# VectorE's order in the projection of a hybrid encoder step: odd side places first, the even place in front of each behind it

## The reference

```python
h = _rms(x, p['norm_gain']) * (1 + scale[:, None, :]) + shift[:, None, :]
(qkv_raw, z_a, beta_raw, alpha_raw, q_raw, ckv_raw, kr_raw, z_b, g_a, g_b) = _split_in(h @ p['w_in'])
o_a, conv_new, s_new = _deltanet(qkv_raw, beta_raw, alpha_raw, conv_buf, s0, p)
o_b, ckv_new, kr_new = _mla(q_raw, ckv_raw, kr_raw, pos, past_ckv, past_kr, p)
```

## Time and profile before

| what | value |
|---|---|
| runs | 1935.47, 1940.38, 1939.29 us; median 1939.29 |
| profiled execution | 1939.42 us, of which the span from first to last instruction 1937.6 us |
| TensorE busy (matmul) | 1806.0 us, 93% of the span |
| VectorE busy | 931.0 us, 48% |
| ScalarE busy | 636.0 us, 33% |
| GpSimd busy | 266.6 us, 14% |
| mean granted TensorE clock | 0.969 |

### The profile page before, as it was taken

One profiled execution on the slowest core, in us unless ns is written; L12 is line 12 of the kernel. 1 busy time (PEld: TensorE's weight loads), 2 busy tenths in 40 slices (PEclk: granted clock), 3 DMA queues, 4 the chain that ended last, 5 costly groups with the idle time before them and its releaser, 6 DMA issues. The chain is left out here.

```text
span 1937.6 us, 28688 instructions
## 1 busy us (share of the span) xinstructions
PE 1806.0 (93%) x11162; PEld 1661.2 (86%) x11162; DVE 931.0 (48%) x1820; ACT 636.0 (33%) x1173; POOL 266.6 (14%) x254
## 2 busy tenths in 40 slices
PE   6899999989888899999999989989999987999898
PEld 2599999989887899999999978878887975999787
DVE  0644455673555486796322144454444556242333
ACT  2322443553433351333333233244333434020100
POOL 0111111434333340241311100000000000000000
PEclk9899999999998999999999989989999987999899
DMA  9322323577775674345654230032251986342222
GB/s 315 116 77 94 102 101 126 170 215 226 221 231 170 184 221 135 126 135 187 214 167 146 112 104 22 28 120 87 77 185 28 368 247 207 131 134 77 100 87 71
DMA packets 235249, 284.06 MB, mean 147 GB/s; under 512 B 42865, under 2 KB 194702, under 8 KB 234988
## 3 DMA queue, kind: packets, MB, share of 16 engines
q1 hardware_dynamic: 233692, 277.82, 44.9%
q10 hardware_dynamic: 1264, 4.39, 0.6%
q0 software_dynamic: 160, 0.05, 0.0%
HBM read 177.30 MB, written 104.92 MB: 146 GB/s over the span
## 5 line engine op out<-in xcount | busy, mean ns | idle before, releaser
L1919 PE MATMUL PS<-HH,WL 128*128 128x352 f32 (+1 forms) x1752 | 392.9, 332 | 4.9 <-DVE mod L2069 4.9
L1919 PE MATMUL PS<-HL,WH 128*128 128x352 f32 (+1 forms) x1752 | 380.6, 326 | 0.0
L1919 PE MATMUL PS<-HH,WH 128*128 128x352 f32 (+1 forms) x1752 | 380.3, 325 | 0.0
L1919 PEld LDWEIGHTS PS<-HH,WH 128*128 128x128 f32 (+1 forms) x1752 | 302.6, 189 | 0.3
L1919 PEld LDWEIGHTS PS<-HH,WL 128*128 128x128 f32 (+1 forms) x1752 | 294.5, 190 | 7.9 <-issue 5.0
L1919 PEld LDWEIGHTS PS<-HL,WH 128*128 128x128 f32 (+1 forms) x1752 | 300.0, 189 | 0.2
L2041 DVE TENSOR_TENSOR WL<-Wraw,WH 128x2048 fp32r<-128x2048 f32 (+1 forms) x37 | 89.7, 2423 | 89.7 <-ACT WH L1691 88.0
L2054 DVE SCALAR_TENSOR_TENSOR R<-R,colA 128x1059 f32<-128x1059 f32 x72 | 99.2, 1378 | 5.9 <-issue 0.5
L1711 ACT ACTIVATE R<-PS 128x1056 f32<-128x1056 f32 (+1 forms) x49 | 51.4, 1050 | 142.4 <-PE PS L1919 142.4
L627 ACT ACTIVATE pr<-PS,amx 128x128 f32<-128x128 f32 (+8 forms) x72 | 51.4, 714 | 132.6 <-DVE amx L661 132.6
L602 PE MATMUL PS<-V,pT 128*128 128x128 f32 (+1 forms) x624 | 86.8, 283 | 3.3 <-ACT pT L639 2.9
(11 more groups left out here) (311 smaller groups left out, 2887.3 us busy)
## 6 DMA issues: line engine op xcount, KB each, us to landing
scratch_proj<-R SPq DMA_DIRECT2D x72, 576.0 KB, 3.3
Wraw<-in_w_in SPq DMA_DIRECT2D x36, 1024.0 KB, 6.9
Wraw<-in_w_ada SPq DMA_DIRECT2D x12, 1024.0 KB, 6.7
job<-scratch_proj SPq DMA_DIRECT2D x18, 512.0 KB, 5.7
fr<-scratch_u SPq DMA_DIRECT2D x16, 528.0 KB, 5.7
gr<-scratch_proj SPq DMA_DIRECT2D x16, 528.0 KB, 3.6
job<-scratch_proj SPq DMA_DIRECT2D x9, 768.0 KB, 6.0
R<-scratch_gcum SPq DMA_DIRECT2D x9, 512.0 KB, 7.0
```

The source lines that it names most:

```text
L1919: last = pe.matmul(PS[0:m, 3 * (p % 2) + b, 0:TB], w[:, u % 2, k, j * P:j * P + m], x[:, k, b * TB:(b + 1) * TB], start=(k == 0 and first) ...
```

## The change

In each w VectorE now takes slot 4w - 1 and then slot 4w - 2 (the even slot of the step before) at the start, and slot 4w + 1 and then slot 4w behind the first half of the inverse. The steps at slots 4w and 4w + 2 where they stood are gone. No operation is added or removed, and no other engine's program is touched.

```diff
         for w in range(NCHUNK + 2):
-            if 4 * w - 1 in side:
-                dve_side(dve, side[4 * w - 1])
+            for slot in (4 * w - 1, 4 * w - 2):
+                if slot in side:
+                    dve_side(dve, side[slot])
...
             if w in dve_steps:
                 dve_decay(dve, dve_steps[w])
-            if 4 * w in side:
-                dve_side(dve, side[4 * w])
...
             for j in inverse_columns(w, 0):
                 eliminate(dve, Xt, Xtmp, HB, j)
-            if 4 * w + 1 in side:
-                dve_side(dve, side[4 * w + 1])
+            for slot in (4 * w + 1, 4 * w):
+                if slot in side:
+                    dve_side(dve, side[slot])
             if w - 1 in periods:
                 differences(periods[w - 1])
             for j in inverse_columns(w, 1):
                 eliminate(dve, Xt, Xtmp, HB, j)
-            if 4 * w + 2 in side:
-                dve_side(dve, side[4 * w + 2])
```

## The result

| | before | after |
|---|---|---|
| median, us (7 runs each) | 1939.29 | 1954.91 |
| lowest and highest, us | 1932.47, 1941.58 | 1946.26, 1959.15 |
| profiled execution, its span, us | 1939.42, 1937.6 | 1959.15, 1957.4 |
| TensorE busy, us | 1806.0 | 1815.6 |
| VectorE busy, us | 931.0 | 922.3 |

The ratio of the times is 1.0086 [1.0061, 1.011]: slower, by 15.6 us between the medians. The profiled execution of after is the highest of its seven runs, so its trace shows 4.2 us more than the median.

A forecast was written before the change was run, and what follows sets the result against it. TensorE was taken to bound the kernel, so only its waits counted; the terms summed to +12.4 us on the profiled 1939.42, giving 1951.8, set at 1951.7 us against the median. The range was 1940 to 1961.

The forecast's parts named there:

- `lb` 1 (-2.2): Behind `kk` 5: its store is issued earlier, so `qk` 5 and `lb` 1 come 2.2 us earlier.
- `lb` 0 and `lb` 4, +5.2 each: `lt` 0 and `lt` 4 delay the differences; `lb` 0 waits 8.3 us instead of 3.1, `lb` 4 likewise 5.2 more.
- `lb` 2, +2.5: Behind `kt` 7: its chain and `lt` 2 both stand in front of `kk` 6, so `lb` 2 waits 2.5 us more.
- SyncE's queue, +2.5: Behind the late output of `lt` 2, decay rows and the store of `kk` 6 queue: 2.5 us at `lt` 3 and `qt` 7.
- `kt` 8, -5.8: The sum of `qt` 7 goes before `lt` 3, so the wait at `kt` 8 goes: 5.8 us gained.
- `lb` 3, +3.0: `lt` 3, stretched by GpSimd's operations, makes the sum of `kt` 8 late; `lb` 3 waits 3.0 us.
- `lb` 7, -3.7: `lt` 6 goes behind the inverse's first columns, eliminations fill idle time, and the wait at `lb` 7 goes: 3.7 us gained.
- `qc` 1 and `qd` 1, +4.85: `qb` 1 behind four operations of the inverse: query norms start later, `qc` 1 and `qd` 1 together come 4.85 us later.
- The clock, +0.9: TensorE's clock falls after long waits: gone at `kt` 8 and `lb` 7, new at `lb` 2, `qc` 1, half at `lb` 3; net +0.9 us.
- The second rival: SyncE's queue after `lt` 2 takes its full 5 us, `lb` 0 and `lb` 4 bring clock falls: about 1958 us; chance 0.14.
- The first rival: Moved chains fall behind GpSimd's operations in chunks 34 to 36 and `qb` 1's rotation, staying short: 1940.7 us; chance 0.18.
- nothing reaches TensorE: Many moves only pass the next slot, so the whole comes to nothing; its chance is counted in the first rival's.

The follow-up runs named there:

- only_t0_t4: Kernel of before with `lt` 0 and `lt` 4 alone moved behind `qk` 4 and `qk` 7; 1951.31 us, ratio 1.0058 to before.
- gains_t3_t6: Kernel of before with `lt` 3 alone moved behind `qt` 7 and `lt` 6 alone behind the first eliminations; 1929.93 us, ratio 0.9952 to before.
- gains_again: The same kernel as gains_t3_t6, timed once more on another chip; 1930.08 us, ratio 0.9953 to before.
- t0_t4_back: Kernel of after with `lt` 0 and `lt` 4 put back in front of `qk` 4 and `qk` 7; 1941.85 us, ratio 1.0016 to before.
- differences_first: Kernel of after with the differences in front of `lt` 0 and `lt` 4, still behind `qk` 4 and `qk` 7; 1958.71 us, ratio 1.0106 to before.

## Why the prediction was right

The forecast was 1951.7 us, slower; it came to 1954.91, inside the range. That the median is so close is in part luck: the execution whose trace the terms are read from took 19.7 us more than the one before, against 12.4, and the projection's last product starts 21.3 us later in it (1142.8 against 1121.5), not some 12. One of the steps failed outright, that of `lb` 1 (-2.2): the jobs between `lb` 0 and `lb` 1 gained nothing. The decay product of `qk` 5, which waits for the store of `kk` 5, in VectorE's timeline of before:
```profile
539.13 1.23 DVE L2147 TENSOR_TENSOR job<-PS,hf 128x1024 f32<-128x1024 f32 x1 [4.26 <-DMA scratch_nl<-job]
```
The decay rows and that store in SyncE's, and the product in VectorE's timeline of after:
```profile
536.09 0.55 SPq L1315 DMA_DIRECT2D R<-scratch_gcum  x1
536.68 0.72 SPq L1320 DMA_DIRECT2D scratch_nl<-job  x1
```
```profile
545.59 1.22 DVE L2145 TENSOR_TENSOR job<-PS,hf 128x1024 f32<-128x1024 f32 x1 [4.64 <-DMA scratch_nl<-job]
```
The store was issued 4.3 us later than the 532.42 of the earlier trace rows, while TensorE's work around it came some 6.3 us later, so the issue had won 2 us. But `qk` 5, released by that store, starts 545.59 - 536.68 = 8.9 us after the issue, where it had taken 539.13 - 532.42 = 6.7 before. The step took an earlier issue for an earlier landing. What did not change is the distance to the decay rows, which stand in front of the store in SyncE's queue: `qk` 5 starts 539.13 - 529.72 = 9.4 us after their issue before and 545.59 - 536.09 = 9.5 in after. The other traces show the same: over twelve executions the store is issued 0.5 to 2.9 us behind the decay rows, and `qk` 5 starts 8.7 to 9.6 us behind them. So the store landed with the transfers in front of it, not with its own issue; no run was made to test this. The other steps:

- **`lb` 0 and `lb` 4, +5.2 each.** Confirmed. `lb` 0 starts 5.4 us later, and only_t0_t4 has the predicted 8.3 us to the digit. In after the wait itself is 6.74, since TensorE arrives later: `qt` 5 waited 1.84 us instead of 0.61 (a wait that differs between executions of one kernel, 0.34 in gains_t3_t6 and 1.75 in gains_again), and took 1.41 us instead of 1.09. At `lb` 4 the release comes 5.5 us later at an equal wait of `qt` 8 (7.07 in only_t0_t4, where `qt` 8 waits 2.32, against 1.53 in t0_t4_back, where it waits 2.29). The 2.4 us at `qt` 8 come with the landing of the store of `kk` 7, not with the move: gains_t3_t6 and gains_again, which are one kernel, have 0.30 and 2.83.
- **`lb` 2, +2.5, and SyncE's queue, +2.5.** Confirmed: 5.11 us at `lb` 2 against 2.65, and 1.19 + 1.49 at `lt` 3 and `qt` 7, where `qt` 7 had waited 0.2 us.
- **`kt` 8, -5.8, and `lb` 3, +3.0.** Confirmed: 0 and 2.70 us. Here the stretching by GpSimd decided, and it was read from the earlier trace rows. The rule of the Trainium skill, "SBUF — State Buffer", Who interferes with whom, stands behind it: a GpSimd instruction in progress blocks fully a VectorE one that needs the shared ports, and the order of issue decides; differences_first shows it with four pairs that end within 0.1 us of each other, apart from the second. The page also says that `tensor_reduce` never contends on trn2, and the sum of 1.22 us beside GpSimd agrees.
- **`lb` 7, -3.7.** Nearly: 0.82 us stayed, 2.9 were won.
- **`qc` 1 and `qd` 1, +4.85.** Confirmed, as a delay. `qa` 1, the job in front, in TensorE's timeline of before and then of after:
```profile
808.68 1.04 PE L1978 MATMUL PS<-cst,job 128*128 128x128 f32 x8
```
```profile
826.03 1.03 PE L1978 MATMUL PS<-cst,job 128*128 128x128 f32 x8
```
From there to `qd` 1, which the rotation releases in both kernels, pass 857.53 - 826.03 = 31.5 us instead of 835.66 - 808.68 = 27.0, 4.5 more. Only 3.88 + 0.21 - 1.35 = 2.7 us of it are waits; the rest fits the clock, 0.91 in the window of 840 to 860 us where that of 820 to 840 had been at 1.00. It filled time in which `qd` 1 would have waited for the rotation, so this fall added nothing to the term.
- **The clock, +0.9.** Mis-sized, and by far the largest miss of the sum. The other terms come to 11.55 us, and TensorE stood still 10.2 us longer over the span. Up to `lb` 7 the waits of the two timelines differ by 9.4 us, where the terms gave 6.7: 1.5 that the jobs around `lb` 1 didn't give, 1.2 at `qt` 8 and `lb` 4 together, and 0.8 that stayed at `lb` 7. Behind it they differ by less than forecast. But the same products kept TensorE busy 9.6 us longer, against 0.9, and 7.2 of this lie in the stretch of the windows above. I had let falls go with `kt` 8 and `lb` 7 and come with `lb` 2, `qc` 1 and, by half, `lb` 3; in after the waits at `lb` 0, `lb` 1, `lb` 2, `lb` 4 and `lb` 5 all leave TensorE at the lower level, and the window around `lb` 0 is at 0.69. The second rival had priced the falls at `lb` 0 and `lb` 4 (3.6 us); they belonged in the forecast. Part of the 9.6 is this execution's own: its mean granted clock is 0.962, that of the median run 0.967.

The first rival (the chains stay short) fell: `lt` 3 was stretched in every kernel that moved it, and the rotation of `qb` 1 took 11.0 us instead of 11.3, which gives back 0.3 and not 2.1. The second, the queue taking its full 5 us, was half right, with 2.7 us at `lt` 3 and `qt` 7. That nothing reaches TensorE fell with the first trace.

## What to carry to other kernels

A chain that stands in an engine's wait for a store is free; moved behind that wait, it costs its whole length to whatever another engine expects from the steps behind it. So before reordering, read for each chain what the engine was idle for in front of the next step, and move only where the engine's own read was late (here `lt` 3 and `lt` 6, which alone make the kernel 0.48% faster). And keep chains of small operations on VectorE away from stretches in which GpSimd works: each GpSimd operation can cost one of them its whole duration. Last, an earlier issue of a store is not an earlier landing: look at what is in front of it in the queue.

## What the runs showed of the hardware

- A chain of some 24 small operations of 0.14 to 0.75 us on VectorE took 5.0 us alone, 8.6 us beside two GpSimd operations and 12.6 us beside four. Cutting the GpSimd operations from 1.9 to 2.6 us down to 0.4 to 0.7 brought it back to 5.4.
- What followed the store of `kk` 5 came 6.7 us after its issue in the kernel before and 8.9 us in after, so that an issue 2 us earlier gained nothing. Counted from the issue of the transfer in front of it, the decay rows, it came after 9.4 and 9.5 us, and in twelve executions after 8.7 to 9.6. That is read from the traces, not tested.
- The length of a wait does not settle the clock behind it. Before, the transposes ran in 0.66 us behind waits of 3.10 us at `lb` 0 and 3.04 at `lb` 1, and in 1.11 us behind 3.09 at `lb` 4; after, in 1.12 us behind 4.47 at `lb` 1, in 0.66 behind 2.70 at `lb` 3 and in 1.11 behind 2.57 at `lb` 5. In gains_t3_t6 the same wait of 3.11 us at `lb` 0 was followed by 1.11 us. Four long waits within 130 us went with a granted clock of 0.91 over 260 us.
